# Raw rows turned by a product with a diagonal of reciprocal norms, in the front of a hybrid decoder layer

## The reference

```python
hn = rms_norm(x, attn_norm_gain[l])          # y = x * rsqrt(mean(x*x) + eps) * gain
proj = hn @ w_in[l]                          # 1024 x 3072, split into q, k, v, cb, cc, cu
attn_o = diff_attention(q, k, v, ...)        # 4 heads, causal, two maps each
conv_o = short_conv(cb, cc, cu, ...)         # norm(cb * conv3(cc * cu))
x = x + jnp.concatenate([attn_o, conv_o], axis=-1) @ w_out[l]
```

## Time and profile before

| | us |
|---|---|
| three runs, median (lowest to highest) | 1182.52 (1179.73 to 1183.26) |
| profiled execution | 1183.22 |
| its span, first to last instruction | 1181.4 |

### The profile page before, as it was taken

One profiled execution on the slowest core, in us unless ns is written; L12 is line 12 of the kernel. 1 busy time (PEld: TensorE's weight loads), 2 busy tenths in 40 slices (PEclk: granted clock), 3 DMA queues, 4 the chain that ended last, 5 costly groups with the idle time before them and its releaser, 6 DMA issues.

```text
span 1181.4 us, 15242 instructions
## 1 busy us (share of the span) xinstructions
PE 1106.2 (94%) x5629; PEld 867.1 (73%) x5629; DVE 841.2 (71%) x1110; ACT 657.1 (56%) x901; POOL 354.9 (30%) x431
## 2 busy tenths in 40 slices
PE   4999999999879999989789999999999999999995
PEld 3998989889658877767657777777777777766663
DVE  6644354343587776766669899889889889888894
ACT  5412121111366555443348778778877877777773
POOL 2432333233311111112104433344344344222220
PEclk9999999999899999999789999999999999999998
DMA  8012030300510222322789999999999999999972
GB/s 243 17 47 61 19 90 1 89 19 18 195 6 19 89 90 90 126 90 98 268 302 355 380 369 373 380 373 366 382 375 369 377 354 356 372 365 360 368 309 44
DMA packets 76506, 254.16 MB, mean 215 GB/s; under 512 B 17808, under 2 KB 42384, under 8 KB 51856
## 3 DMA queue, kind: packets, MB, share of 16 engines
q1 hardware_dynamic: 69264, 236.37, 54.0%
q0 software_dynamic: 7168, 16.79, 6.0%
HBM read 240.55 MB, written 20.97 MB: 221 GB/s over the span
## 4 chain that ended last, share of the span: by engine, by line
PE 43%; DMA 7%; DVE 3%; ACT 1%; issue 1%; POOL 0%; POOLq 0%; SPq 0%; ACTq 0%; DVEq 0%
PE banks L2070 9%; PE banks L2072 9%; PE banks L2071 9%; PE banks L2089 4%; PE banks L2091 4%; PE banks L2087 4%; DMA raw<-in_w_up 3%; DMA raw<-in_w_gate 3%; PE banks L2046 2%; DVE wlo L1991 1%; PE banks L2055 1%; DMA rows<-xn_rows,table_i 1%; ACT whi L1940 1%; DMA xn_rows<-hn 0%; PE banks L1611 0%
## 5 line engine op out<-in xcount | busy, mean ns | idle before, releaser
L1991 DVE TENSOR_TENSOR wlo<-raw,whi 128x2048 fp32r<-128x2048 f32 x190 | 428.0, 2287 | 52.2 <-ACT whi L1940 52.0
L1940 ACT CAST whi<-raw 128x2048 fp32r<-128x2048 f32 x188 | 354.0, 1910 | 39.0 <-DMA raw<-in_w_gate 23.5
L2070 PE MATMUL banks<-whi,rT_hi 128*96 128x512 f32 x512 | 206.9, 404 | 7.1 <-DVE wlo L1991 6.1
L1922 POOL DMA_INDIRECT out<-y_sb,table_i x32 | 150.5, 4702 | 198.1 <-ACT y_sb L1958 192.9
L2072 PE MATMUL banks<-whi,rT_lo 128*96 128x512 f32 x512 | 203.0, 396 | 0.0
L2071 PE MATMUL banks<-wlo,rT_hi 128*96 128x512 f32 x512 | 201.8, 394 | 0.0
L2070 PEld LDWEIGHTS banks<-whi,rT_hi 128*96 128x96 f32 x512 | 83.1, 162 | 43.2 <-DVE wlo L1991 7.2
L2072 PEld LDWEIGHTS banks<-whi,rT_lo 128*96 128x96 f32 x512 | 82.9, 162 | 36.4
L1913 POOL DMA_INDIRECT rows<-xn_rows,table_i x30 | 52.4, 1745 | 188.7 <-PE banks L2046 181.1
L2071 PEld LDWEIGHTS banks<-wlo,rT_hi 128*96 128x96 f32 x512 | 83.4, 163 | 31.4
L847 ACT ACTIVATE qk_sq<-banks 128x256 f32<-128x256 f32 x32 | 12.3, 385 | 150.0 <-PE banks L1469 150.0
(11 more groups left out here) (248 smaller groups left out, 2051.1 us busy)
## 6 DMA issues: line engine op xcount, KB each, us to landing
raw<-in_w_gate SPq DMA_DIRECT2D x64, 1024.0 KB, 22.1
raw<-in_w_up SPq DMA_DIRECT2D x64, 1024.0 KB, 22.4
raw<-in_w_down SPq DMA_DIRECT2D x64, 1024.0 KB, 23.6
c_raw<-in_w_in SPq DMA_DIRECT2D x12, 512.0 KB, 3.8
q_raw<-in_w_in SPq DMA_DIRECT2D x12, 512.0 KB, 6.0
x_stage<-in_x SPq DMA_DIRECT2D x8, 512.0 KB, 7.7
wo_raw<-in_w_out SPq DMA_DIRECT2D x2, 2048.0 KB, 10.4
h_sb<-in_x SPq DMA_DIRECT2D x8, 512.0 KB, 4.6
```

What stands on the lines that cost most here:

```text
L1922: pool.indirect_dma_start(out=s.out_rows, out_offset=bass.IndirectOffsetOnAxis(ap=s.table_i[:, e:e + 1], axis=0), in_=s.y_sb[e % 2][:], in ...
L1940: act.copy(s.w_hi[i % HI][:], s.raw[i % RING][:]).then_inc(s.hi_ready, 1)
L1991: dve.tensor_tensor(s.w_lo[i % RING][:], s.raw[i % RING][:], s.w_hi[i % HI][:].bitcast(F32), ALU.subtract).then_inc(s.lo_ready, 1)
L2070: pe.matmul(o, s.rT_hi[e % 2][:, c, :], hi[:, c4, :], start=(c == 0), stop=False)
```

## The change

x is no longer normalised on DVE. POOL multiplies the identity by the tile's reciprocal norms, and PE multiplies the raw rows by this diagonal: the product is the transposed tile with its norms. The gain of the norm belongs to a channel and so goes into the weights: round_q, low_q, round_c and low_c now multiply by gain1_c, one instruction for each of eight chunks. The waits for q_lo go chunk by chunk in the first projection of a head. The order changes too: only tile 0 is turned ahead of project(0), each later tile inside the projection (or unit) before, unit 0 stands behind project(3) and unit 1 behind project(4); all tiles use the same two PSUM banks; q of head 0 is loaded right behind x tile 0 and the gain, and nine small loads stand between x tile 1 and tile 2. The low half of a conv block waits for all its eight high chunks.

The diff, with what only renames or drops unused names left out:

```diff
--- before.py
+++ after.py
@@ -34,9 +34,8 @@
-PIECES = 4
...
-UNIT_AFTER = (-1, 2, 5, 6, 7, 7, 9, 11, 13, 14, 15, 15, 17, 19, 21, 22, 23, 23, 25, 26, 28, 29, 31, 31)
+UNIT_AFTER = (3, 4, 5, 6, 7, 7, 9, 11, 13, 14, 15, 15, 17, 19, 21, 22, 23, 23, 25, 26, 28, 29, 31, 31)
...
@@ -177,8 +176,8 @@
-        xn = [at(f"xn{b}", 72 + 8 * b, [P, D]) for b in range(2)]
-        gain1 = at("gain1", 88, [P, D])
+        diag_x = [at(f"diag_x{b}", 72 + 8 * b, [P, P]) for b in range(2)]
+        gain1_c = at("gain1_c", 3.8125, [P, KC])
...
@@ -466,7 +464,7 @@
     def units_after(p):
...
-        return [n for n in range(1, UNITS) if UNIT_AFTER[n] == p]
+        return [n for n in range(UNITS) if UNIT_AFTER[n] == p]
...
     def split_after(n):
...
@@ -505,8 +503,15 @@
     def x_banks(t):
...
-        a = 6 if t in (1, 3) else 4
-        return a, ps[:, a:a + 2, :]
+        return 4, ps[:, 4:6, :]
...
+    def turned_in(p):
...
+        return {0: 1, 1: 2, 2: 3, 3: 4, 4: 6}.get(p)
...
+    def turned_in_unit(n):
...
+        return {0: 5, 1: 7}.get(n)
...
     def quad(a):
...
@@ -578,7 +579,7 @@
         def _(sp):
             def load_x(t):
-                sp.dma_start(s.x_stage[t][:], s.x_rows[t * P:(t + 1) * P, :]).then_inc(x_in[(t + 2) // 2 if t > 1 else t], 16)
+                sp.dma_start(s.x_stage[t][:], s.x_rows[t * P:(t + 1) * P, :]).then_inc(x_in[t], 16)
...
             def load_q(h):
...
@@ -595,20 +596,22 @@
-                sp.dma_start(s.gain1[:], s.attn_norm_gain[0:1, :].to_broadcast([P, D])).then_inc(gain1_in, 16)
-                for t in range(1, 4):
-                    load_x(t)
-                load_c(0)
+                sp.dma_start(s.gain1_c[:], s.attn_norm_gain[0].rearrange("(c p) -> p c", p=P)).then_inc(gain1_in, 16)
                 load_q(0)
+                load_x(1)
...
-                for t in range(4, NT):
+                load_x(2)
+                load_x(3)
+                load_c(0)
+                load_x(4)
+                load_c(1)
+                for t in range(5, NT):
...
-                load_c(1)
...
@@ -670,7 +673,12 @@
             def rstd_x(t):
...
-                pool.tensor_tensor(s.rstd_x[:, t:t + 1], s.ss_x[:, t:t + 1], s.neg_half[:, t:t + 1], ALU.pow).then_inc(x_rstd_ready, 1)
+                own.then(pool.tensor_tensor(s.rstd_x[:, t:t + 1], s.ss_x[:, t:t + 1], s.neg_half[:, t:t + 1], ALU.pow))
+                if t == 0:
+                    pool.wait_ge(consts, 1)
+                if t >= 2:
+                    pool.wait_ge(x_turned, t - 1)
+                pool.tensor_scalar(s.diag_x[t % 2][:], ident[:], s.rstd_x[:, t:t + 1], None, ALU.mult).then_inc(diag_ready, 1)
...
             def rotate(p):
...
@@ -747,21 +755,20 @@
-            for t in range(4):
-                rstd_x(t)
...
+            rstd_x(0)
...
-            rstd_x(4)
-            rstd_x(5)
+            rstd_x(1)
             for p in range(PROJ):
+                if p < 4:
+                    rstd_x(p + 2)
                 rotate(p)
                 rstd_qk(p)
-                if p < 2:
-                    rstd_x(6 + p)
+                if 3 <= p < 5:
+                    rstd_x(p + 3)
...
@@ -816,13 +823,13 @@
         def _(act):
             def square_x(t):
-                act.wait_ge(x_in[(t + 2) // 2 if t > 1 else t], 32 if t > 1 else 16)
+                act.wait_ge(x_in[t], 16)
...
             def round_x(t):
-                act.wait_ge(xn_turned, t + 1)
+                act.wait_ge(x_turned, t + 1)
...
@@ -830,14 +837,19 @@
-                for n in range(PIECES):
-                    act.copy(piece(s.q_hi, n), piece(s.q_raw, n).rearrange("p c j n -> p c (j n)")).then_inc(q_hi_ready, 1)
+                if h == 0:
+                    act.wait_ge(gain1_in, 16)
+                for c in range(KC):
+                    act.activation(s.q_hi[:, c, :], s.q_raw[:, c, :, :].rearrange("p j n -> p (j n)"), ACT.Identity,
+                                   scale=s.gain1_c[:, c:c + 1]).then_inc(q_hi_ready, 1)
...
             def round_c(j):
...
-                act.copy(s.c_hi[j % 2][:], s.c_raw[j % 2][:]).then_inc(c_hi_ready, 1)
+                for c in range(KC):
+                    act.activation(s.c_hi[j % 2][:, c, :], s.c_raw[j % 2][:, c, :], ACT.Identity,
+                                   scale=s.gain1_c[:, c:c + 1]).then_inc(c_hi_ready, 1)
...
             def take_projection(p):
...
@@ -947,33 +959,32 @@
-            square_x(1)
...
-            square_x(2)
...
-            square_x(3)
-            for t in range(1, 4):
-                round_x(t)
-            round_c(0)
...
-            square_x(4)
-            square_x(5)
-            copy_c(0)
-            round_c(1)
+            square_x(1)
             for p in range(PROJ):
+                if turned_in(p) is not None:
+                    round_x(turned_in(p))
+                if p < 4:
+                    square_x(p + 2)
                 take_projection(p)
-                if p < 4:
-                    round_x(4 + p)
-                if p < 2:
-                    square_x(6 + p)
+                if 1 <= p < 3:
+                    round_c(p - 1)
...
+                if p == 4:
+                    square_x(7)
...
                     round_k(p - 2)
                 for n in units_after(p):
+                    if turned_in_unit(n) is not None:
+                        round_x(turned_in_unit(n))
+                    if n < 1:
+                        square_x(6)
...
@@ -1054,13 +1065,6 @@
-            def normalise(t):
-                dve.wait_ge(x_rstd_ready, t + 1)
-                if t >= 2:
-                    dve.wait_ge(xn_turned, t - 1)
-                dve.scalar_tensor_tensor(s.xn[t % 2][:], s.x_stage[t][:], s.rstd_x[:, t:t + 1], s.gain1[:],
-                                         ALU.mult, ALU.mult).then_inc(xn_ready, 1)
...
             def low_x(t):
...
@@ -1068,15 +1072,16 @@
             def low_q(h):
-                for n in range(PIECES):
-                    dve.wait_ge(q_hi_ready, PIECES * h + n + 1)
-                    dve.tensor_tensor(piece(s.q_lo, n), piece(s.q_raw, n).rearrange("p c j n -> p c (j n)"),
-                                      piece(s.q_hi, n).bitcast(F32), ALU.subtract).then_inc(q_lo_ready, 1)
+                for c in range(KC):
+                    dve.wait_ge(q_hi_ready, KC * h + c + 1)
+                    dve.scalar_tensor_tensor(s.q_lo[:, c, :], s.q_raw[:, c, :, :].rearrange("p j n -> p (j n)"), s.gain1_c[:, c:c + 1],
+                                             s.q_hi[:, c, :].bitcast(F32), ALU.mult, ALU.subtract).then_inc(q_lo_ready, 1)
...
             def low_c(j):
-                dve.wait_ge(c_hi_ready, j + 1)
-                dve.tensor_tensor(s.c_lo[j % 2][:], s.c_raw[j % 2][:], s.c_hi[j % 2][:].bitcast(F32),
-                                  ALU.subtract).then_inc(c_lo_ready, 1)
+                dve.wait_ge(c_hi_ready, KC * (j + 1))
+                for c in range(KC):
+                    dve.scalar_tensor_tensor(s.c_lo[j % 2][:, c, :], s.c_raw[j % 2][:, c, :], s.gain1_c[:, c:c + 1],
+                                             s.c_hi[j % 2][:, c, :].bitcast(F32), ALU.mult, ALU.subtract).then_inc(c_lo_ready, 1)
...
             def apply_gain(p):
...
@@ -1317,36 +1322,25 @@
-            normalise(0)
-            normalise(1)
-            low_x(0)
-            normalise(2)
-            low_x(1)
-            normalise(3)
-            low_x(2)
-            low_x(3)
-            low_c(0)
-            low_q(0)
-            normalise(4)
...
+            low_x(0)
+            low_q(0)
...
-            normalise(5)
-            low_c(1)
             for p in range(PROJ):
+                if turned_in(p) is not None:
+                    low_x(turned_in(p))
...
                     scale_qk(p - 1)
                 apply_gain(p)
                 sum_squares(p)
-                if p < 4:
-                    low_x(4 + p)
-                if p < 2:
-                    normalise(6 + p)
+                if 1 <= p < 3:
+                    low_c(p - 1)
...
@@ -1354,6 +1348,8 @@
                 for n in units_after(p) if p < PROJ - 1 else ():
+                    if turned_in_unit(n) is not None:
+                        low_x(turned_in_unit(n))
...
@@ -1447,23 +1443,27 @@
         def _(pe):
             def turn_x(t):
...
-                pe.wait_ge(xn_ready, t + 1)
-                if t >= 2:
-                    pe.wait_ge(xlo_ready, t - 1 if t < 5 else t)
+                pe.wait_ge(diag_ready, t + 1)
+                if t >= 1:
+                    pe.wait_ge(xlo_ready, t)
...
-                    ins = pe.transpose(ps[:, a + c // 4, (c % 4) * P:(c % 4 + 1) * P], s.xn[t % 2][:, c * P:(c + 1) * P], ident[:])
-                ins.then_inc(xn_turned, 1)
+                    ins = pe.matmul(ps[:, a + c // 4, (c % 4) * P:(c % 4 + 1) * P], s.x_stage[t][:, c * P:(c + 1) * P], s.diag_x[t % 2][:],
+                                    start=True, stop=True)
```

(24 more changed lines are left out.)

7 lines of the change are left out of this document (3 added, 4 removed).

## The result

Six runs of the changed kernel have a median of 1192.26 us (1188.95 to 1194.67), six of the kernel before on the same chip 1182.39. The ratio is 1.0081, with a 95% interval of 1.0059 to 1.0104: slower by 9.9 us, where the forecast had 5.2 and a range up to 1191.5. In a later session the ratio was 1.0091 [1.0074, 1.0108]. The profiled execution took 1194.67, its span 1192.9.

A forecast was written before the change was run, and what follows sets the result against it. PE was taken as busy for 94% of the span, its start held by a chain over ACT, DVE and POOL. Milestone 6.1 later, later heads -0.9: 5.2 slower, 1187.7 us beside the median of 1182.52, range 1184.5 to 1190.5.

The forecast's parts named there:

- The earlier start: Front of PE: project(0) starts at 14.8, tile 1 is turned at 19.6, project(1) starts at 24.0.
- the case of the slow power of 1.44: POOL, tile 1's norm: a power of 0.58 alone took 1.44 during a DVE operation; upper bound for tile 1 20.0.
- The turning: PE, turn_x: eight products take 1.79, 1.0 more a tile than transposes; tile 0's take 3.6 at the lower clock.
- Rival D: PE, turn_x: a product with the diagonal costs like a transpose, 0.79 a tile; 1178.7 us, faster; chance 0.08.
- From project(1) to the milestone: PE, until tiles 0-7, projections 0-4, units 0-1 are done: 39.7 plus 4.25 of waits; ends at 67.95, 6.1 later.
- rival B: PE in unit 1: the clock falls in the wait of 3.5 for tile 7; chance 0.25.
- A: The forecast itself for the whole kernel: 1187.7 us, range 1184.5 to 1190.5; chance 0.50.
- The later heads: Later heads: b blocks' low halves add 2.7, q_lo waits piece by piece save 3.6; together -0.9.
- The fourth comes earlier than its unit: Later heads, b blocks: 0.9 more at three of four blocks, since the fourth is ready earlier than its unit.
- The sum: Whole kernel: 6.1 at the milestone minus 0.9 in later heads gives 5.2 us slower.
- The other signs: Profile after: among others, c_lo waits of 0.9 before units 4, 10, 16, and projection 5's first matmul near 68.
- rival C: Front loads come late: q weights after 12.9 or tile 2 after 22.7; +1 to +3, 1189.5 us; chance 0.12.

The follow-up runs named there:

- g2: Changed kernel with tile 7's square and norm early, b blocks' low halves early, and products replaced by raw transposes (norms left out): 1174.40 us, ratio 0.9940.
- f4: Kernel before with q_lo waits piece by piece and the first conv block split before tile 3 is finished: 1175.80 us, ratio 0.9938.
- e3: Changed kernel with each tile's eight products replaced by transposes of the raw rows, norms left out of the result: 1183.20 us, ratio 1.0001.
- g1: Kernel before with only the q_lo waits made piece by piece in projections 0, 8, 16 and 24: 1178.53 us, ratio 0.9963.
- g3: f4 with 16 unread matmuls of 512 columns ahead of turn_q(2), in PE's wait of 3.91 us: 1176.39 us, ratio 0.9945.
- g4: Kernel before with the change's order, tile 7 early and q_lo in pieces, but rows normalised on DVE and transposed: 1175.04 us, ratio 0.9946.
- e1: Changed kernel with square_x(7) ahead of take_projection(4) on ACT and rstd_x(7) ahead of rotate(4) on POOL: 1184.35 us, ratio 1.0013.
- e2: Changed kernel with 16 unread matmuls of 512 columns ahead of the wait for tile 7's diagonal: 1193.76 us, ratio 1.0067.
- e4: Kernel before with 37 extra unread matmuls of 512 columns behind unit 0: 1190.51 us, ratio 1.0054.
- f1: Changed kernel run again without any edit: 1194.29 us, ratio 1.0091.
- f2: Changed kernel with DVE's low halves of the b blocks moved ahead of the previous unit's own work: 1191.34 us, ratio 1.0063.
- f3: Changed kernel with tile 7's square and norm early and the b blocks' low halves early: 1184.72 us, ratio 1.0011.

## Why the prediction was wrong, point by point

**The earlier start: right, 0.5 short.** Project(0) came 0.23 late, tile 1 0.5 and project(1) 0.5. The term that was mis-sized is the diagonal on POOL. I took 0.35 for it, "near the row of the same shape", the select of 0.29; it takes 0.61 to 0.62, above even the upper bound of 0.58. On tile 0 that hid behind a load that landed 0.3 earlier (the square began at 5.33, not 5.64). For tile 1 it is most of the loss: the square began at 17.05 instead of 16.8, and then came 0.28 + 0.57 + 0.61 with the hand-overs, 1.8 instead of 1.3. POOL's power ran from 18.72, when DVE's gain pieces had ended at 18.58, and took 0.57, so the case of the slow power of 1.44 did not come up here; the scaling before it, which overlapped the last of those pieces, took 0.28 where its rows shown above have 0.19. The start of tile 1 was 20.11, just above the upper bound of 20.0, but through the diagonal's price.

**The turning: right.** Eight products step in 1.70 to 1.81 at full clock, forecast 1.79; tile 0 took 3.75, forecast 3.6 at the lower clock. Rival D, the product at the price of a transpose, is out, and g2 puts the whole at 7.06 net.

**From project(1) to the milestone: the failed step.** Forecast 43.95 (39.7 and 4.25 of waits), measured 70.72 - 24.50 = 46.22. The waits are as forecast in sum and in place, by their rows: 0.11, 0.48, 0.12 and 3.60. What is missing is 1.7 of clock: tile 7 at 3.21 instead of 1.77 (1.45), and the unit's next matmul at a step of 0.53 instead of 0.31 (0.2). The sum of the forecast had PE go on at full clock behind the wait and put this term at nothing; rival B, with 0.25, was this fall. The rows of the kernel before give its price: unit 0 took 7.34, its matmuls 0.43 apart up to 27.65 and 0.23 apart from 27.97 on, against 5.57 for unit 5, so 1.8. The other 0.5 is in the waits too: from step to step each is 0.15 to 0.25 longer than its row, which makes 5.04 of the four (six matmuls into project(1), PE goes from 25.48 to 25.92, where a step is 0.17 and the wait in the row 0.11), and tiles 2 to 6 gave 0.2 of that back, 8.72 where 8.95 was forecast.

Was 0.25 a fair weight? The earlier trace rows had one wait of 3.91 with a fall and one of 3.70 without, and I took the case as open between the two. The same waits in all 14 profiles, and the two other long ones of before's trace behind its start, say more (a fall is a granted clock below 1.00 at the end of the wait or within 2 us behind it):

| PE's wait | releaser | profiles with it | clock fell |
|---|---|---|---|
| 2.58 | h_sb | 14 | 14 |
| 3.48 | wlo | 14 | 9 |
| 3.60 | tile 7's diagonal | 4 | 4 |
| 3.70 | o_sb | 11 | 10 |
| 3.91 | q_dup | 13 | 13 |

The one case of 3.70 without a fall, which the forecast leaned on, is the odd one out of eleven. The busy times of the 4 us behind that wait in before, in the changed kernel and in f4 (granted clock 1.00, 0.68 and 0.50), with PE's row in f4:

```profile
330.10:334.10 4.00, 3.98 (x25) 3.04 (x25) 3.59 (x6) 3.47 (x7) 0.00 (x0) 1.00 0.02 4
```
```profile
338.40:342.40 4.00, 3.95 (x21) 3.30 (x21) 3.54 (x6) 3.51 (x7) 0.00 (x0) 0.68 0.00 0
```
```profile
324.30:328.30 4.00, 4.00 (x16) 3.50 (x17) 3.51 (x6) 3.44 (x7) 0.00 (x0) 0.50 0.00 0
```
```profile
324.30 0.47 PE L1573 MATMUL banks<-ident,o_sb 128*128 128x128 f32 x1 [3.70 <-DVE o_sb L1161]
```

What PE did ahead of that wait was the same in all eleven (busy for the whole 2.4 us before it, and for 0.67 of the 1.6 before that), so neither the length of the wait nor the work ahead of it explains the odd one. The 3.48 says the same from the other side: PE is busy for all 4 us ahead of it in all 14, and in five of them, before's among them, the clock stayed up. Length doesn't order the cases either, since 2.58 always had a fall. So before's trace alone held two falls and two waits without one, and didn't call for B over A; but reading one wait without a fall as a place where the clock stays was reading one execution's luck. By the 56 cases of the table, 50 of them with a fall, a fall had the better odds by far. What decides in a single case stays open.

**The later heads: two terms right, one missing.** Three waits of 0.90, as forecast, and those for q_lo gone. "The fourth comes earlier than its unit" was right for the fourth b block; but the block of unit 19 was not checked and waits 0.84. With the overlap that rows hide, the heads gave back 0.38 instead of 0.9.

**The sum.** At the start of attention: 0.5 (start) + 1.7 (clock) + 0.5 (the part of the waits that rows leave out) + 0.5 (heads) = 3.2, and 5.2 + 3.2 = 8.4 against 8.46 measured at attention. From there to 9.87 in the median is no more than the interval (7.0 to 12.3). Of the profiled execution's 11.5, 3.2 come after PE's last matmul on gathered rows: PE waited 3.53 for hid in the last expert, where the kernel before has 1.78, and then worked at a lower clock (a row of its timeline, and the busy times of 4.4 us from there, granted clock 0.61):

```profile
1172.08 0.55 PE L2051 MATMUL banks<-ident,hid 96*128 96x96 f32 x4 [3.53 <-DVE hid L1998]
```
```profile
1172.00:1176.40 4.40, 4.32 (x15) 3.02 (x16) 2.61 (x3) 0.48 (x1) 0.00 (x0) 0.61 0.00 0
```

Whether the change favours that is open. The stretch from that matmul's start to the end took 41.4 to 43.0 in the seven profiles with a wait of 1.8 there (before, e3, f4, g1 to g4) and 44.6 to 46.1 in the seven with one of 3.2 to 3.9 (changed, e1, e2, e4, f1 to f3); e4, which is the kernel before with a delay, is among the slow ones and f3, whose attention starts as in before, too. It was not tried by itself.

**The other signs.** The loads were in time (rival C): no wait of ACT for q or tile 2. The granted clock below 1 behind the wait, named as B's sign, was there.

## What to carry to other kernels

An operation that is moved to the front of a chain has to be moved ahead on each queue that it passes: here both ACT and POOL had idle time for tile 7 and did it behind projection 4; the place of these two calls was worth 5.8 of the 8.5 us at the start of attention. A wait of some 3.5 us on TensorE is to be priced with the slow clock behind it as the likelier case (behind the waits of 3.48 to 3.91 us in these 14 profiles the clock fell in 36 of 42), and one trace without a fall is no evidence against it. Such a fall cost 1.7 us at tile 7, where TensorE's next work was on the path, but nothing to be seen in attention, whose stretch up to the expert table took 272.8 in before without a fall behind the wait of 3.70 and 272.7 in the changed kernel with one. And when a change bundles a costly part with cheap ones, try the cheap ones on the old kernel: waits for a buffer piece by piece gave 4.4 us there, and together with one swap in ACT's and DVE's order 7.3.

## What the runs showed of the hardware that was not expected

- At the start of a program the granted clock and the durations disagree. The windows of f1 give 1.00 for all of 8 to 31 us, yet in its PE timeline the matmuls of projection 0 step at 0.32 from 15.41 to 18.61 and tile 1, at 20.21, takes 3.65; from 23.87 on the same matmuls step at 0.17, and tile 2, at 27.65, takes 2.05. Where a window does give 0.50, the slow values stand: in the changed kernel's first profile 0.32 a matmul from 15.67 to 18.23 (0.50 from 15.6 to 19.0) and 3.56 for tile 7 (0.50 from 63.4 to 66.8). So the durations are what I go by at the front.
- By these durations two executions of one program reach the full clock at different points: in f1 tile 1, at 20.21, takes 3.65, in the changed kernel's first profile, at 20.11, 2.02; unit 0 took 6.90 in f4 (22.85 to 29.75) and 7.87 in g3 (22.89 to 30.76), whose front is the same code. The starts of attention lie 1.5 apart in the first pair and 1.1 in the second, so I estimate that up to some 1.5 us of a milestone can be this alone.
- A tensor_scalar of a 128x128 fp32 tile took 0.61 to 0.62 on POOL for all eight diagonals of the changed kernel (0.67 once each in e1 and e2), a select of the same shape 0.29, fp32 or bf16.
- Behind one and the same wait in the same stream of work the clock fell in some executions and not in others: 9 of 14 for 3.48 us, 10 of 11 for 3.70; and it fell behind 2.58 us in 14 of 14.
- The waits of TensorE that I followed from step to step were 0.15 to 0.25 longer than their rows say, since matmul ends are modelled (1.14 against 0.90 ahead of unit 4). The four between project(1) and the milestone add up to 4.31 in the rows and to 5.04 from step to step, so a sum over rows is too low.
